# A gated decoder block on one core: the first block of x loaded ahead of the first half weight, and transposes of probabilities ahead of the next scores in two attention steps of each pair

## The reference, cut to what matters

```
h = rms_norm(x, pre_mix_g);  proj = h @ w_in          # q, k, v, u_pool, u_conv, gate logits
attn = softmax(q k^T / 8 + bias, causal) v, 8 heads of 64     # 512 tokens: all past blocks are taken
pool = pool_mixer(u_pool) @ w_pool_o;  conv = conv_module(u_conv) @ w_conv_o
merged = sum of sigmoid(gate_i) * branch_i
x = x + rms_norm(merged @ w_out, post_mix_g)
x = x + rms_norm((silu(g) * up) @ w_ffn_out, post_ffn_g)      # g, up = rms_norm(x) @ w_ffn_in
```

## Time and profile before

| | |
|---|---|
| median of three runs | 698.02 us (697.25 to 698.41) |
| profiled execution | 697.11 us, span of its instructions 695.0 us |
| TensorE matmuls | 687.5 us busy, 99% of the span |
| weight loads | 608.8 us, 88% |
| VectorE | 548.4 us, 79% |
| ScalarE | 364.8 us, 52% |
| GpSimd | 234.4 us, 34% |
| granted TensorE clock, mean | 0.998 of full speed |

### The profile page before, as it was taken

How to read it: one execution, slowest core, us unless ns; L and a number is a source line. 1 busy time by engine, 2 the same in 40 slices (tenths; PEclk the granted TensorE clock), 3 DMA queues, 4 the chain that set the end, 5 groups by cost and what they waited for, 6 DMA issues and landing times.

```text
span 695.0 us, 10966 instructions
## 1 busy us (share of the span) xinstructions
PE 687.5 (99%) x3983; PEld 608.8 (88%) x3983; DVE 548.4 (79%) x801; ACT 364.8 (52%) x590; POOL 234.4 (34%) x206
## 2 busy tenths in 40 slices
PE   9999999999999999999999999999999999999996
PEld 7888888888888888888889999999999999888885
DVE  6584889778876666886479988888888787888997
ACT  7552555545546555233456555455445545656673
POOL 0845221222222000670224465556557640000123
PEclk9999999999999999999999999999999999999999
DMA  8534999989997523226302313312332234565563
GB/s 348 188 110 135 259 232 229 257 205 257 217 225 208 139 90 121 92 91 228 136 31 92 117 66 121 121 70 111 121 121 75 106 121 154 197 196 192 175 206 139
DMA packets 38562, 109.43 MB, mean 157 GB/s; under 512 B 4016, under 2 KB 4152, under 8 KB 38336
## 3 DMA queue, kind: packets, MB, share of 16 engines
q1 hardware_dynamic: 30512, 85.90, 35.6%
q0 software_dynamic: 8000, 23.07, 15.6%
q10 hardware_dynamic: 16, 0.00, 0.0%
HBM read 106.85 MB, written 25.19 MB: 190 GB/s over the span
## 4 chain that ended last, share of the span: by engine, by line
PE 99%; POOL 0%; DVE 0%; POOLq 0%; DVEq 0%; ACT 0%; issue 0%; ACTq 0%
PE bank L1745 31%; PE bank L1747 31%; PE bank L1746 31%; PE bank L1837 1%; PE bank L1827 1%; PE bank L1828 1%; PE bank L1848 1%; PE bank L1847 1%; PE bank L1976 1%; PE bank L1772 0%; PE bank L1761 0%; PE bank L1775 0%; PE bank L1778 0%; PE bank L1765 0%; PE bank L1860 0%; PE bank L1867 0%
## 5 line engine op out<-in xcount | busy, mean ns | idle before, releaser
L1745 PE MATMUL bank<-h_hi,w_hi 128*128 128x512 f32 (+1 forms) x312 | 118.2, 379 | 0.0
L1747 PE MATMUL bank<-h_hi,w_lo 128*128 128x512 f32 (+1 forms) x312 | 116.5, 374 | 0.0
L1746 PE MATMUL bank<-h_lo,w_hi 128*128 128x512 f32 (+1 forms) x312 | 116.4, 373 | 0.0
L1128 DVE TENSOR_TENSOR w_lo<-raw,w_hi 128x1024 fp32r<-128x1024 f32 x53 | 70.4, 1330 | 31.8 <-ACT w_hi L675 31.3
L1747 PEld LDWEIGHTS bank<-h_hi,w_lo 128*128 128x128 f32 x312 | 58.8, 188 | 10.6
L1745 PE MATMUL bank<-tm_hi,blk_hi 128*128 128x256 f32 x240 | 68.0, 283 | 0.0
L1746 PE MATMUL bank<-tm_lo,blk_hi 128*128 128x256 f32 x240 | 68.0, 283 | 0.0
L1747 PE MATMUL bank<-tm_hi,blk_lo 128*128 128x256 f32 x240 | 68.0, 283 | 0.0
L1746 PEld LDWEIGHTS bank<-h_lo,w_hi 128*128 128x128 f32 x312 | 58.8, 189 | 9.7
L1745 PEld LDWEIGHTS bank<-h_hi,w_hi 128*128 128x128 f32 x312 | 58.8, 188 | 9.5
L1568 DVE TENSOR_TENSOR blk_lo<-raw_pair,blk_hi 128x512 fp32r<-128x512 f32 (+1 forms) x40 | 60.4, 1509 | 8.4 <-ACT blk_hi L987 8.4
(11 more groups left out here) (279 smaller groups left out, 1884.7 us busy)
## 6 DMA issues: line engine op xcount, KB each, us to landing
raw<-in_w_in_dram SPq DMA_DIRECT2D x41, 512.0 KB, 5.2
raw_pair<-in_w_ffn_in_dram SPq DMA_DIRECT2D x40, 512.0 KB, 3.9
comb<-in_w_ffn_out_dram POOLq DMA_DIRECT2D x30, 512.0 KB, 7.6
raw<-comb SPq DMA_DIRECT2D x20, 512.0 KB, 3.6
raw<-in_w_ffn_out_dram SPq DMA_DIRECT2D x15, 512.0 KB, 3.8
comb<-comb POOLq DMA_DIRECT2D x10, 512.0 KB, 4.6
raw<-in_w_branch_dram SPq DMA_DIRECT2D x8, 512.0 KB, 3.2
raw<-in_w_out_dram SPq DMA_DIRECT2D x8, 512.0 KB, 3.3
```

The source lines that it names most:

```text
L1128: dve.tensor_tensor(dst, src_hi[0], src_hi[1], ALU.subtract).then_inc(lo_done, 1)
L1745: pe.matmul(dst, a_hi, b_hi, start=start, stop=False, skip_group_check=resumed)
L1746: pe.matmul(dst, a_hi, b_lo, start=False, stop=False, skip_group_check=resumed)
L1747: return pe.matmul(dst, a_lo, b_hi, start=False, stop=stop, skip_group_check=resumed)
```

## The change

On SP's queue `xg` part 0 is issued ahead of the first half weight, where it was issued between the two halves. Two of the six identity transposes after the turn of the gains are left out. In steps 3 and 4 of each pair, `turn_probs` of the two groups stands ahead of `scores` of the next two. In the last pair the wait for the variance row moves with the transposes. Nothing else is changed, on no other engine.

```
             for half, signal in enumerate((raw_half, raw_full[0])):
-                if half:
+                if not half:
                     xg_load(0)
                 cols = slice(half * SEQ, (half + 1) * SEQ)
...
             pe.transpose(bank[6][:, 0:KT], g_rows[0:KT, :], ident[0:KT, 0:KT]).then_inc(g_turned, 1)
-            for _ in range(6):
+            for _ in range(4):
                 pe.transpose(bank[7][:, 0:P], ident[:, :], ident[:, :])
...
                 if j == 3:
-                    scores(p, 2)
-                    scores(p, 3)
                     if last:
                         pe.wait_ge(ln_dve, 4)
                     turn_probs(p, 0)
                     turn_probs(p, 1)
+                    scores(p, 2)
+                    scores(p, 3)
                 if j == 4:
+                    turn_probs(p, 2)
+                    turn_probs(p, 3)
                     scores(p, 4)
                     scores(p, 5)
-                    turn_probs(p, 2)
-                    turn_probs(p, 3)
                     if last:
```

## The result

Over 19 runs of each kernel the median went from 698.02 to 699.6 us (698.72 to 700.5): the ratio is 1.0021, with a 95% interval of 1.0015 to 1.0027, so by the ratio +1.5 us (1.0 to 1.9), a slowdown of 0.2% that the noise doesn't hide. The forecast was 699.7.

A forecast was written before the change was run, and what follows sets the result against it. TensorE's full stream of matmuls was taken as the bound. 1.77 (step 3) - 0.05 (step 4) + 0 (start) gave +1.72 us, carried to the 698.02 median as 699.7 us, range 698.5 to 700.8.

The forecast's parts named there:

- What bounds the kernel: TensorE holds 99% of the chain, longest wait 0.4 us; an added wait is paid whole unless a later one swallows it.
- Step 3: Transposes of probabilities 0 and 1 wait on VectorE's normalising in pairs 0 to 2: 0.59, 0.60, 0.58, together +1.77 us.
- the bare weight load: At the waiting transposes of step 3: a weight load with no matmul to hide it, 0.10 us of each wait.
- VectorE tied to TensorE: From step 1 to step 3's normalising, VectorE follows TensorE's K unit through ScalarE, so the wait returns in each pair.
- Rival (a): VectorE keeps its own pace, so only pair 0's wait is paid: +0.6 us, 698.6; chance 0.11.
- (b): No transpose waits and the start's 0.28 us is kept: -0.3 us, 697.7; chance 0.05.
- Step 4 covered by step 3: In step 4 TensorE arrives late from step 3, so transposes don't wait on the normalising: -0.05 us, from pair 0.
- Rival (c): Both steps pay: pair 0's 0.55 and pair 2's 0.50 us in step 4 are added, +2.8, 700.8; chance 0.07.
- Sum: Whole kernel: 1.77 - 0.05 + 0 = +1.72 us, 699.7 at the median; chance 0.72.
- The start: First real matmul 0.28 us earlier, near 4.70, but TensorE then waits longer for unit 1's low part: 0 us.
- the forecast's own signs: Profile after: wrong if one wait, waits in step 4, a start gap moving everything, or span growth outside 1.2 to 2.2 us.
- Rival (d), the clock: At the start TensorE's clock rises some eight matmuls later: +1.1 us on top, 700.8; chance 0.05.

The follow-up runs named there:

- step 4 alone: Transposes ahead of scores only in step 4, start and step 3 as before, against the kernel before: 698.79 us (697.92 beside it), ratio 1.0012.
- the two kernels with moved taps: Kernel before with VectorE's convolution instructions of step 2 moved behind step 3's normalising: 697.41 us with transposes first in steps 3 and 4, 698.03 with scores first (698.05 before).
- step 3 alone: Transposes ahead of scores only in step 3, start and step 4 as before, against the kernel before: 699.42 us (697.92 beside it), ratio 1.0020.
- taps moved, scores first: Kernel before with VectorE's convolution instructions of step 2 moved behind step 3's normalising, TensorE's order unchanged: 698.03 us (698.05 beside it), ratio 0.9998.

## Why the prediction was right

By its steps:

- **What bounds the kernel.** Right: a wait put into TensorE's stream is paid nearly in whole. The wait of the earlier trace rows kept its 0.4 us and swallowed nothing; only the small waits of step 4 did.
- **Step 3.** Right in place, number of waits and cause: waits in pairs 0 to 2, none in pair 3. The size was 0.56 us by weight loads (0.55 by matmuls) for each, not 0.59: 1.63 over the pairs, not 1.77. The term that was mis-sized is the bare weight load, 0.10 in the sum: from the end of the normalising at 85.24 to the scores' stream at 85.57 (their load at 85.46 and 0.11 more) there are 0.33 us, of which two transposes take 0.22 and the signal 0.06, so some 0.05 are left for it.
- **VectorE tied to TensorE.** Right: the wait returned in pairs 1 and 2 at the same 0.60 us. The chain in the profile after shows the tie itself: ahead of each of the three waits it comes off TensorE at `k_hi` (line 850, 73.54 in pair 0), which is made from the K unit's result, and runs by VectorE and ScalarE to the normalising. Rival (a), a single payment, falls, and so does (b), no wait at all.
- **Step 4 covered by step 3.** Right, and shown from both sides: no wait in the changed kernel, 1.3 us of waits with step 4 alone. The -0.05 was right as well, for the reason given (the seven transposes went from 0.98 to 0.93 in pair 0); the same effect in pair 2, 0.03 us, was left out. Rival (c), both pay, falls.
- **Sum.** 1.72 was forecast, 1.55 lie between the marks and 1.58 between the medians. Step 3 paid 1.63 where 1.77 stood in the sum, and step 4 gave back 0.08 where 0.05 did. The order itself seems to save some hundredths of a microsecond a pair, as the two kernels with moved taps suggest; that was not in the sum, and why it would isn't shown.
- **The start.** 0 was right at the median (ratio 0.9999 alone), and so was the reason, a head start that ends in the wait for unit 1's low part. Wrong was what the profile after would show, a first real matmul near 4.7 and the one at 11.07 unmoved: in the profiled execution they stood at 5.49 and 13.01. The forecast took the landings of one trace as fixed. They aren't: with the start as before, the first mark stood between 27.53 and 29.16 in nine traces, and with the changed start at 27.90 and 29.33. The trace of the kernel before had the earliest of all, 1.0 below the middle one of the nine, which fits that its execution (697.11) lay 0.91 us below the median. So carrying the 0.91 over was right, but the forecast's own signs, applied to the profile after, would have called it wrong: the gap at the start moved everything, and the span grew from 695.0 to 698.4, by 3.4 us and not by 1.2 to 2.2. Only the medians and the marks show that the mechanism held.
- **What sets the start.** From ScalarE's start on the third load of x (line 699) to the first mark it takes 20.07 to 20.12 us in ten of the eleven traces, whatever TensorE did before: this landing alone sets it, as the forecast's chain said. The eleventh is the profile after, with 20.67 (29.33 - 8.66). Of its 1.80 us over the kernel before, 1.24 are thus the landing (8.66 against 7.42), and 0.56 are TensorE's late start, by the late half weight and the slow matmuls.
- **Rival (d), the clock.** It did show in the profiled execution, and there it cost at most these 0.56 us, not 1.1. The traces' records of the granted clock reach the full level at 9.70 us from the span's start in it, at 6.15 in the kernel before, at 6.57 with only the start changed, and anywhere from 4.77 to 7.75 in the nine traces with the start as before. The Trainium skill ("TensorE: Matmul & The Clock Gate", "What's actually happening") says that the clock follows how busy the engine has been, so fewer dummies may bring a later rise. The latest of the eleven rises does stand with the changed start, but the other trace with that start is among the middle ones, so two traces can't say whether it is made likelier. Up to 7.75 the moment made no difference to the first mark. The latest rise with the start as before is that of step 3 alone; the earliest is that of taps moved, scores first, which has full pace nearly from its first real matmul and still the latest first mark but one, since its third load of x was taken up last (9.07). Their rows, in this order:

```profile
6.82 1.51 PE L1775 MATMUL bank<-w_lo,x_hi_a 128*128 128x512 f32 x4
...
5.14 1.16 PE L1772 MATMUL bank<-w_hi,x_hi_a 128*128 128x512 f32 x4
...
9.07 1.34 ACT L699 ACTIVATE x_hi_a<-xg,g_cols 128x512 fp32r<-128x512 f32 x2 [1.24 <-DMA xg<-in_x_cols_dram]
```

What stays open: the hundredths of a microsecond a pair of the order, and how often the clock rises late.

## What to carry to other kernels

Where two short pieces of work on the bounding engine change places, read at what moment the input of each is ready, not how long they take: the piece put first must have its input there, and 0.8 us of other work can be all that hides a 0.55 us producer. Whether several such waits add up depends on what the producer follows. The three of step 3 did add up, at 0.4 to 0.5 us a pair, since VectorE's work starts anew from a TensorE result in each pair. Those of step 4 vanished behind those of step 3, since TensorE had been made late and the producer had not; there the cost was the larger of the two and not their sum, and undoing the edit of step 4 brought nothing back. Compare traces between marks inside the kernel: of 3.3 us between the two profiled executions here, 1.8 came from the start.

## What the runs showed that I had not expected

The start of one and the same order of loads varies by 1.6 us (first mark 27.53 to 29.16, nine traces): the third load of x is taken up by ScalarE anywhere from 7.42 to 9.07, and the first mark follows it by 20.1 us each time, whether the clock rises at 4.77 or at 7.75. And moving work on an engine that is busy 79% of the time, without a change on the bounding one, was worth 1.65 us, as it made that engine's result early at three places.
